# Smaller blocks in the merges of a triangular inverse and in the last two score levels

## The reference, cut to what matters

```python
A = jnp.where(strict, jnp.einsum('bhncd,bhnsd->bhncs', kb, k) * decay, 0.0)
uw = lax.linalg.triangular_solve(A + eye, rhs, left_side=True, lower=True, unit_diagonal=True)
```

```python
decay = jnp.exp(jnp.where(causal, diff, -jnp.inf))
A = jnp.einsum('bhcsd,bhsd->bhcs', q_n[:, :, :, None, :] * decay, k_n)
```

## Time and profile before

| | |
|---|---|
| time, median of 3 runs | 1238.33 us (1238.32 to 1238.42) |
| profiled execution, its own time | 1237.48 us |
| span of its trace, first to last instruction | 1235.6 us |
| TensorE busy | 1192.2 us (96%) |
| VectorE, ScalarE, GpSimd busy | 538.0, 509.2, 429.3 us |
| mean granted TensorE clock | 0.986 |

### The profile page before, as it was taken

One profiled execution on the slowest core, in us unless ns is written; L12 is line 12 of the kernel. 1 busy time (PEld: TensorE's weight loads), 2 busy tenths in 40 slices (PEclk: granted clock), 3 DMA queues, 4 the chain that ended last, 5 costly groups with the idle time before them and its releaser, 6 DMA issues.

```text
span 1235.6 us, 16722 instructions
## 1 busy us (share of the span) xinstructions
PE 1192.2 (96%) x6668; PEld 1006.1 (81%) x6668; DVE 538.0 (44%) x859; ACT 509.2 (41%) x653; POOL 429.3 (35%) x334
## 2 busy tenths in 40 slices
PE   5889999999999999999989999999999999999997
PEld 4557877888888888888779888888888878999986
DVE  1464333434442154657843446722200533553535
ACT  4245444444421135764433424555322353324541
POOL 0014443455444452433411311033444346333320
PEclk9889999999999999999989999999999999999999
DMA  9993322322233332314141212013242332222201
GB/s 351 386 331 120 102 73 98 102 88 82 102 122 102 102 102 103 95 43 137 34 137 34 69 34 102 1 35 103 81 139 98 102 107 76 96 69 69 69 1 69
DMA packets 108577, 128.76 MB, mean 104 GB/s; under 512 B 13275, under 2 KB 99041, under 8 KB 108385
## 3 DMA queue, kind: packets, MB, share of 16 engines
q1 hardware_dynamic: 103412, 120.69, 29.4%
q10 hardware_dynamic: 5101, 7.15, 1.7%
HBM read 122.58 MB, written 5.24 MB: 103 GB/s over the span
## 4 chain that ended last, share of the span: by engine, by line
PE 50%; issue 31%; POOL 14%; DMA 1%; DVE 1%; SPq 1%; ACT 1%; ACTq 0%; POOLq 0%
PE ps L270 14%; PE ps L271 14%; PE ps L272 14%; POOL wl L397 13%; PE ps L2253 2%; PE ps L1626 2%; PE ps L1671 1%; PE ps L1608 1%; DMA ada<-in_ada_w 1%; DMA pool_band<-in_pool_band 1%; PE ps L2274 1%; PE ps L1697 1%; SPq L304 0%; PE ps L2276 0%; PE ps L2264 0%
## 5 line engine op out<-in xcount | busy, mean ns | idle before, releaser
L397 POOL TENSOR_TENSOR wl<-raw,wh 128x512 fp32r<-128x512 f32 x312 | 409.9, 1346 | 776.9 <-ACT wh L432 776.9
L270 PE MATMUL ps<-xth,wh 128*128 128x512 f32 (+1 forms) x832 | 327.3, 393 | 5.0 <-DVE xtl L1063 3.4
L272 PE MATMUL ps<-xth,wl 128*128 128x512 f32 (+1 forms) x832 | 319.1, 383 | 0.0
L271 PE MATMUL ps<-xtl,wh 128*128 128x512 f32 (+1 forms) x832 | 319.0, 383 | 0.0
L432 ACT ACTIVATE wh<-raw 128x2048 fp32r<-128x2048 f32 x78 | 149.2, 1912 | 344.0 <-PE ps L272 318.3
L270 PEld LDWEIGHTS ps<-xth,wh 128*128 128x128 f32 x832 | 157.7, 190 | 38.4 <-issue 7.7
L272 PEld LDWEIGHTS ps<-xth,wl 128*128 128x128 f32 x832 | 157.5, 189 | 31.2
L271 PEld LDWEIGHTS ps<-xtl,wh 128*128 128x128 f32 x832 | 157.9, 190 | 28.1 <-issue 0.2
L1074 DVE SCALAR_TENSOR_TENSOR conv_out<-ps,conv_taps,conv_out 128x511 f32<-128x511 f32 x44 | 32.8, 744 | 139.3 <-ACT conv_out L575 139.3
L270 PE MATMUL ps<-wh,xth 128*128 128x256 f32 (+1 forms) x304 | 92.0, 303 | 0.1
L272 PE MATMUL ps<-wh,xtl 128*128 128x256 f32 (+1 forms) x304 | 91.2, 300 | 0.0
(11 more groups left out here) (310 smaller groups left out, 1734.5 us busy)
## 6 DMA issues: line engine op xcount, KB each, us to landing
ada<-in_ada_w SPq DMA_DIRECT2D x24, 1024.0 KB, 10.7
raw<-in_gdn_w_in SPq DMA_DIRECT2D x24, 1024.0 KB, 5.2
raw<-in_ffn_w_up SPq DMA_DIRECT2D x22, 1024.0 KB, 4.9
raw<-in_gla_w_in SPq DMA_DIRECT2D x12, 1024.0 KB, 5.0
raw<-in_ffn_w_down SPq DMA_DIRECT2D x11, 1024.0 KB, 4.9
raw<-in_gdn_w_out SPq DMA_DIRECT2D x8, 1024.0 KB, 4.9
raw<-in_gla_w_out SPq DMA_DIRECT2D x4, 1024.0 KB, 5.0
xres<-in_x SPq DMA_DIRECT2D x4, 512.0 KB, 5.4
```

Of the source, the lines that this page charges most:

```text
L270: nc.tensor.matmul(o, lh, rh, start=first, stop=False)
L271: nc.tensor.matmul(o, lh, rl, start=False, stop=False)
L272: return nc.tensor.matmul(o, ll, rh, start=False, stop=last)
L397: rest = nc.gpsimd.tensor_tensor(lo[:, part], raw[:, s, part], hi[:, part].bitcast(f32), ALU.subtract)
```

## The change

In level 6 the transpose takes only the upper left 64x64 block, and both products only the 64x64 blocks that matter. In level 5 the transpose stays whole, and each 128x128 product becomes two products on 64 rows, `r` = rows 0 to 63 and 64 to 127, written to different partitions. ScalarE copies only what is used. In the scores, item 6 (level 5) computes two 32x32 blocks per chunk and head, item 7 (level 6) one 64x64 block; items 0 to 5 stay.

```diff
@@ -667,14 +667,21 @@
             def turned_copy(i, level):
 
                 act.wait_ge(S("x0_mm"), 4 * (i // 2) + i % 2 + 1 + (2 if level == 6 else 0))
-                nc.scalar.activation(turned_inv[:, i % 2], bank2(4 + 2 * (i % 2)).rearrange("p (h n) -> p h n", n=P), ACT.Copy)\
-                    .then_inc(S("yt_done"), 1)
+                x0 = bank2(4 + 2 * (i % 2)).rearrange("p (h n) -> p h n", n=P)
+                if level == 6:
+                    nc.scalar.activation(turned_inv[0:64, i % 2, :, 0:64], x0[0:64, :, 0:64], ACT.Copy).then_inc(S("yt_done"), 1)
+                else:
+                    nc.scalar.activation(turned_inv[0:64, i % 2, :, 0:32], x0[0:64, :, 0:32], ACT.Copy)
+                    nc.scalar.activation(turned_inv[64:128, i % 2, :, 0:32], x0[64:128, :, 64:96], ACT.Copy).then_inc(S("yt_done"), 1)
 
             def prod_copy(i, level):
 
                 act.wait_ge(S("p1_mm"), 4 * (i // 2) + i % 2 + 1 + (2 if level == 6 else 0))
-                nc.scalar.activation(prods[i % 2][:], bank2(4 + 2 * (i % 2)).rearrange("p (h n) -> p h n", n=P), ACT.Copy)\
-                    .then_inc(S("prod_done"), 1)
+                p1 = bank2(4 + 2 * (i % 2)).rearrange("p (h n) -> p h n", n=P)
+                if level == 6:
+                    nc.scalar.activation(prods[i % 2][64:128, :, 0:64], p1[64:128, :, 0:64], ACT.Copy).then_inc(S("prod_done"), 1)
+                else:
+                    nc.scalar.activation(prods[i % 2][:, :, 0:32], p1[:, :, 0:32], ACT.Copy).then_inc(S("prod_done"), 1)
 
             def w_copy(i):
 
@@ -2006,7 +2013,10 @@
                     else:
                         pe.wait_ge(S("w_done"), 1)
                 for h in range(H):
-                    mm = turn(head2(b, h), tinv[:, i, h, :])
+                    if level == 6:
+                        mm = turn(head2(b, h)[0:64, 0:64], tinv[0:64, i, h, 0:64], 64)
+                    else:
+                        mm = turn(head2(b, h), tinv[:, i, h, :])
                 mm.then_inc(S("x0_mm"), 1)
 
             def level_first(i, level):
@@ -2014,7 +2024,12 @@
                 n = 4 * (i // 2) + i % 2 + (3 if level == 6 else 1)
                 pe.wait_ge(S("yt_done"), n)
                 for h in range(H):
-                    mm = X.matmul(head2(4 + 2 * (i % 2), h), neg[:, i, h, :], turned_inv[:, i % 2, h, :], start=True, stop=True)
+                    o = head2(4 + 2 * (i % 2), h)
+                    if level == 6:
+                        mm = X.matmul(o[64:128, 0:64], neg[0:64, i, h, 64:128], turned_inv[0:64, i % 2, h, 0:64], start=True, stop=True)
+                    else:
+                        for r in (slice(0, 64), slice(64, 128)):
+                            mm = X.matmul(o[r, 0:32], neg[r, i, h, r], turned_inv[r, i % 2, h, 0:32], start=True, stop=True)
                 mm.then_inc(S("p1_mm"), 1)
 
             def level_second(i, level):
@@ -2022,7 +2037,13 @@
                 n = 4 * (i // 2) + i % 2 + (3 if level == 6 else 1)
                 pe.wait_ge(S("prod_done"), n)
                 for h in range(H):
-                    mm = X.matmul(head2(4 + 2 * (i % 2), h), prods[i % 2][:, h, :], tinv[:, i, h, :], start=True, stop=True)
+                    o = head2(4 + 2 * (i % 2), h)
+                    if level == 6:
+                        mm = X.matmul(o[0:64, 64:128], prods[i % 2][64:128, h, 0:64], tinv[64:128, i, h, 64:128], start=True, stop=True)
+                    else:
+                        for r in (slice(0, 64), slice(64, 128)):
+                            m, n = slice(r.start, r.start + 32), slice(r.start + 32, r.stop)
+                            mm = X.matmul(o[m, n], prods[i % 2][r, h, 0:32], tinv[r, i, h, n], start=True, stop=True)
                 mm.then_inc(S("yy_mm"), 1)
 
             def turn_keys_of(i):
@@ -2250,8 +2271,16 @@
                 for h in range(LH):
                     for tt in range(TT):
                         c = slice(tt * P, (tt + 1) * P)
-                        mm = X.matmul(ps[:, 4 + h, c], (kg if j == 0 else zg)[:, h, c], (qg if j == 0 else zg)[:, h, c],
-                                      start=True, stop=True)
+                        early, late = slice(tt * P, tt * P + 64), slice(tt * P + 64, (tt + 1) * P)
+                        if j == LEVELS - 1:
+                            for a in (tt * P, tt * P + 64):
+                                s = a % P
+                                mm = X.matmul(ps[s:s + 32, 4 + h, a + 32:a + 64], zg[:, h, a:a + 32], zg[:, h, a + 32:a + 64], start=True, stop=True)
+                        elif j == LEVELS:
+                            mm = X.matmul(ps[0:64, 4 + h, late], zg[:, h, early], zg[:, h, late], start=True, stop=True)
+                        else:
+                            mm = X.matmul(ps[:, 4 + h, c], (kg if j == 0 else zg)[:, h, c], (qg if j == 0 else zg)[:, h, c],
+                                          start=True, stop=True)
                 mm.then_inc(S("lev_mm"), 1)
 
             for tt in range(TT - 1):
```

## The result

The changed kernel takes 1222.65 us (median of 4 runs, 1221.84 to 1223.59), the kernel before 1238.32 us beside it (4 runs, 1237.95 to 1238.42). The ratio is 0.9874 [0.9857, 0.9891], 15.7 us less. The forecast was 1223.9. The profiled execution took 1222.44 us, its span is 1220.6 us.

What follows compares the result with a forecast made beforehand. The prediction took TensorE to bound the kernel. Gains of 11.8 us in the merges, 1.9 in item 6 and 0.7 in item 7 sum to 14.4, from 1237.48 to 1223.1, plus 0.85 for the median: 1223.9 us, range 1221.5 to 1232.

Steps and rivals of the forecast that it cites:

- What bounds the kernel: Whole kernel: TensorE bounds it, busy for 1192.2 of 1235.6 us; the merges stand in its time and other engines have slack.
- The size: Whole kernel: all gains of the merges and the scores together sum to 14.4 us.
- Level 5, first product: Merges, each pair of chunks: 2.13 us for 3.57, a gain of 1.44, taken as 1.2.
- Rival 2: Level 5 products: tiles on different rows take turns; the sum is 11.3, so 1227.0 us. Chance 0.18.
- Level 5, second product, and level 6 transposes: Merges, each pair of chunks: a gain of 1.8 us, limited by waiting for VectorE's last copy of level 5.
- Level 6 products: Merges, each pair of chunks: first and second product each 2.13 us for 3.57, a gain of 1.44 each.
- Rival 4: 64-column tiles: the weight load isn't hidden, 0.11 us a half; sum 2.1, so 1236.2 us. Chance 0.05.
- Item 6: Scores, level 5 blocks: 1.24 us for 3.57, a gain of 2.3, taken as 1.9.
- Rival 3: All small blocks: each half has a floor of 0.058 us whatever its size; sum 5.1, so 1233.2 us. Chance 0.12.
- Item 7: Scores, level 6 block: 2.13 us for 3.57, but only 0.7 gained, as the second chunk's product waits for ScalarE's gates.
- Rival 6: Behind the merges: half of the gain comes back as waits for ScalarE or VectorE, near 1231 us. Chance 0.09.
- Rival 5: Behind the 12 light blocks: TensorE's clock falls, losing 18 us if every block brings a fall, 1241.9 us. Chance 0.04.

Runs made afterwards that it cites:

- one tile kernel: Against the changed kernel, level 5 makes both products of a head on rows 0 to 63 and leaves out rows 64 to 127; 1227.81 us (one run).
- Level 6 alone: Against the kernel before, only the level 6 merge works on blocks, level 5 and the scores stay; ratio 0.9956, 1231.71 us.

## Why the prediction was right

**What bounds the kernel: right.** The busy time of TensorE fell by 15.6 us and the time by 15.7.

**The size: 14.4 us forecast, 15.0 between the profiled executions.** The 0.6 are two terms that I cut for caution, 0.2 in each pair for level 5's first product and 0.3 for item 6. The forecast of the median is 1.25 us too high; the other half of that is the 0.85 us by which the kernel before had its median above its profiled execution, and which is 0.2 in the changed kernel.

**Level 5, first product: right, a little low.** The two starts, of this product and of the second, are 6.31 us apart before and 4.94 now: 1.37 gained in each pair, where I had worked out 1.44 and taken 1.2 because no row showed such a sequence. The step is 0.058 us (0.056 assumed), the way in and out as priced. Rival 2, row tiles in turn, falls for this pair of tiles with the one tile kernel. The Trainium skill, "TensorEngine Tiling (Array Packing)", restrictions and gotchas, says that different row tiles can't access the same PSUM bank simultaneously. Here the two tiles of a head write to one bank, on different partitions, and 64 halves took 1.99 us where one tile took 3.84: the measurement speaks against that rule for such a pair.

**Level 5, second product, and level 6 transposes: right.** From the start of the one to the start of level 6's first product it is 11.72 us before and 9.93 now: 1.79 for 1.8. (The terms that the prediction names, 657.26 + 0.45 + 0.19, make 657.90 and not 657.97, a gain of 1.9; the extra 0.07 is named nowhere.) VectorE's copies are the bound, as forecast: with the transposes moved behind them the merges gain 1.0 us more in each pair. What I had missed is that the waits cost more than their rows, so moving the transposes paid 2.03 and not the 1.4 that I expected of it.

**Level 6 products: right.** 1.38 and 1.44 for 1.44 each. Rival 4 (3.9 us a block) falls with 2.01. Level 6 alone gave 6.54 for 6.8.

**Item 6: the term was mis-sized.** I had worked out 2.3 us and cut it to 1.9 for caution; it gains 15.08 - 12.84 = 2.24 from its start to that of item 7. The rows:

```profile
1132.15 0.28 PE L272 MATMUL ps<-wh,xtl 128*128 128x256 f32 x1
1132.36 1.21 PE L2278 MATMUL ps<-zg 128*32 128x32 f32 x64
1133.49 0.39 PE L270 MATMUL ps<-wh,xth 128*128 128x256 f32 x1
1133.71 0.28 PE L271 MATMUL ps<-wl,xth 128*128 128x256 f32 x1
```

The block takes 1.13 us, and with 0.09 ahead of it and 0.10 behind it (0.21 and 0.22 where 0.12 is normal) the detour costs 1.32, where 1.24 was worked out: the step is 0.032 us, 0.029 was assumed. Rival 3, a floor of 0.058 for each half, falls with it: 64 halves start in 1.13 us, 0.018 each. The Trainium skill, "TensorE: Matmul & The Clock Gate", on the gap between back-to-back matmuls, has a floor of about 25 ns between starts. If it held across two tiles, the block would take 1.6 us at least; it takes 1.13, with starts in pairs 7 ns apart, so it doesn't hold there. Within one tile no half here came closer than 31 ns, so no run tests it. (Rows 8, which the prediction set against it, are starts of weight loads and not of products.)

**Item 7: right.** From its start to the output products 8.76 us before, 8.02 now: 0.74, or 0.65 with its way in, for 0.7, with the wait on `gg` where it was expected.

**Rival 6** (half given back) did not come: the only new waits are the two that the sum holds. **Rival 5** was priced as unlikely because, among other things, the blocks last only 2 us. The runs bear that out, with less room than I had thought: in one tile and at less than twice the length the clock fell in two blocks of four.

## What to carry to other kernels

A product of which only a block is needed is worth cutting down when TensorE bounds the kernel. The time of an fp32 half followed the columns of its weights (0.109, 0.058, 0.032 us for 128, 64, 32), here with a moving operand no wider than that: with 64 columns of weights it was 0.058 us for 64 and for 32 moving columns. A detour to a tile cost about 0.2 us more, so cut whole groups, not single products. The two tiles of a head overlapped fully only when they alternated in the program. Then look for the work that the shorter product now reaches too early, and move it on: two edits of order here gave 2.8 us more in the merges and scores.

## What the runs showed of the hardware

- Two 64x64 tiles on different rows and columns run side by side (64 halves in 1.99 us for 3.84 in one tile), also where both write to one PSUM bank on different partitions.
- With tile after tile in the program, a change of tile let only three to four halves start early (0.2 us at 0.058 a step).
- The granted clock can fall to 1.2 GHz while TensorE is busy without a gap. Where level 5's first product ran in one tile at a time it fell inside both blocks of 128 halves, behind one of two of 3.84 us and near the end of one of two of 3.2 to 3.4 us. It fell behind no block of 2.0 us, and in neither of two of 3.85 us in two tiles.
- A wait for another engine cost TensorE more than its row in two places: 0.42 us for a row of 0.25, and 0.73 for a row of 0.46.
